# Two token blocks and the first weight slice of the second layer's projections fetched, split and multiplied during the last output tile of the first layer

## What is computed

```python
for i in range(DEPTH):                       # two layers, D_MODEL = 1024
    hp = rms_norm(xp, norm_g[i])
    if i % 2 == 0:
        zp = hp @ w_in_pool[j]               # 1024 x 4096
        br_p = pool_mix(u_p_ext, pos_p, w_pool_grp[j], pool_scale[j])
    else:
        zp = hp @ w_in_sb[j]                 # 1024 x 7168
        br_p = stick_breaking(q_p, k_p, v_p, pos_p, pos_p, sb_bias[j])
    xp = xp + merge_out(br_p, gate_p, mq_p, mg_p, mk_p, mv_p, mem_q_g[i], w_out[i])
```

## Time and profile before

| | us |
|---|---|
| three runs | 2331.37, 2334.16, 2334.32 |
| median | 2334.16 |
| profiled execution | 2338.4 |
| its span | 2336.7 |
| TensorE busy in the span | 2201.2 (94%) |
| mean granted TensorE clock | 0.971 |

### The profile page before, as it was taken

One profiled execution on the slowest core, in us unless ns is written; L12 is line 12 of the kernel. 1 busy time (PEld: TensorE's weight loads), 2 busy tenths in 40 slices (PEclk: granted clock), 3 DMA queues, 4 the chain that ended last, 5 costly groups with the idle time before them and its releaser, 6 DMA issues. The chain is left out here.

```text
span 2336.7 us, 47103 instructions
## 1 busy us (share of the span) xinstructions
PE 2201.2 (94%) x18709; PEld 1834.6 (79%) x18709; DVE 1292.6 (55%) x2040; ACT 1009.2 (43%) x2090; POOL 433.0 (19%) x542
## 2 busy tenths in 40 slices
PE   7799999997999689999999998889999999998999
PEld 6799899886688589999999997766666566654787
DVE  6846666435422374334444443588888888875211
ACT  7533223215311144333333343457777777775100
POOL 0533223202000043222222221321121111100000
PEclk9899999998899889999999999889999999999999
DMA  8222222144635553334433336789999999978331
GB/s 289 86 87 89 79 64 66 66 166 163 210 119 155 146 186 102 109 99 133 153 106 109 96 96 234 253 292 379 396 407 393 406 395 388 375 284 307 123 108 55
DMA packets 283274, 453.98 MB, mean 194 GB/s; under 512 B 30962, under 2 KB 208062, under 8 KB 283038
## 3 DMA queue, kind: packets, MB, share of 16 engines
q1 hardware_dynamic: 274958, 421.83, 51.8%
q0 software_dynamic: 8000, 29.10, 3.3%
q10 hardware_dynamic: 96, 0.02, 0.0%
HBM read 372.43 MB, written 78.43 MB: 193 GB/s over the span
## 5 line engine op out<-in xcount | busy, mean ns | idle before, releaser
L233 DVE TENSOR_TENSOR h_w_lo<-l_w,h_w_hi 128x512 fp32r<-128x512 f32 x264 | 213.7, 811 | 221.2 <-ACT h_w_hi L226 218.7
L226 ACT ACTIVATE h_w_hi<-l_w 128x512 fp32r<-128x512 f32 x264 | 166.7, 633 | 239.9 <-PE i_c L322 81.4
L320 PE MATMUL i_x<-h_t_hi,h_w_hi 128*128 128x264 f32 x560 | 163.3, 292 | 6.8 <-DVE h_t_lo L279 6.8
L2960 PEld LDWEIGHTS b_krow<-ar_arena,b_qd 128*32 128x32 f32 x3072 | 107.2, 111 | 72.6 <-issue 57.0
L192 POOL TENSOR_TENSOR h_w_lo_full<-l_w 128x512 f32<-128x512 f32 x44 | 57.5, 1308 | 560.5 <-DMA l_w<-in_w_in_sb_dram 229.9
L320 PE MATMUL i_y<-h_t_hi,h_w_hi 128*128 128x264 f32 x560 | 161.3, 288 | 0.0
L322 PE MATMUL i_x<-h_t_hi,h_w_lo 128*128 128x264 f32 x560 | 161.0, 287 | 0.0
L321 PE MATMUL i_x<-h_t_lo,h_w_hi 128*128 128x264 f32 x560 | 160.4, 286 | 0.0
L321 PE MATMUL i_y<-h_t_lo,h_w_hi 128*128 128x264 f32 x560 | 159.0, 284 | 0.0
L322 PE MATMUL i_y<-h_t_hi,h_w_lo 128*128 128x264 f32 x560 | 158.9, 284 | 0.0
L2960 PE MATMUL b_krow<-ar_arena,b_qd 128*32 128x128 f32 x3072 | 140.7, 279 | 7.9 <-ACT b_kev L2666 6.9
(11 more groups left out here) (368 smaller groups left out, 6424.9 us busy)
## 6 DMA issues: line engine op xcount, KB each, us to landing
ar_arena<-in_cache_sb_k_dram SPq DMA_DIRECT2D x73, 768.0 KB, 9.7
bf_vpage<-in_cache_sb_v_dram SPq DMA_DIRECT2D x64, 768.0 KB, 8.8
b_vpage<-in_cache_sb_v_dram SPq DMA_DIRECT2D x64, 768.0 KB, 8.5
l_w<-in_w_in_sb_dram SPq DMA_DIRECT2D x56, 512.0 KB, 3.9
l_w<-in_cache_sb_k_dram SPq DMA_DIRECT2D x36, 768.0 KB, 9.4
l_w<-in_w_in_pool_dram SPq DMA_DIRECT2D x32, 512.0 KB, 4.2
bf_kpage<-in_cache_sb_k_dram SPq DMA_DIRECT2D x19, 768.0 KB
ar_arena<-scratch_yT SPq DMA_DIRECT2D x14, 1024.0 KB, 6.6
```

The source lines that it names most:

```text
L226: act.activation(self.w_hi[:, i % RING, :, :], self.source(i), ACT.Copy).then_inc(self.high, 1)
L233: dve.tensor_tensor(self.w_lo[:, i % RING, :, :], self.source(i), self.w_hi[:, i % RING, :, :].bitcast(F32), ALU.subtract).then_inc(self.r ...
L320: pe.matmul(out, w_hi, t_hi, start=kk == 0 and x in ("P1", "P2", "P5"), stop=False, skip_group_check=True)
L2960: ins = pe.matmul(krow[pair * CT:(pair + 1) * CT, 0:P], qd[:, i % 2, at:at + CT], kt[u % 2][:, h, f, :], start=odd == 0 and f == 0, stop=o ...
```

## The change

Blocks 0 and 1 and slice a of the second layer's first pair are loaded by SyncE in the output phase, in the turn of tile 7 behind that tile's `load_other`. New places in SBUF are given to them, at addresses that tile 7 reads no more once its third weight row has been used (semaphore `dead`). ScalarE and VectorE round and split the two blocks and the weights of P1 and P2 at the end of the turn of tile 6. TensorE does P1 and the first half of P2 between the last output product and the transposes of tile 7, and the second half of P2 behind them. The order of the first pair becomes P1, P2, P5, and `in_phase` begins with P5. There the list of loads is shorter by slice a and blocks 0 and 1, and slice a of the second pair no longer waits for the split of the P3 weights, since the first pair's a lies elsewhere. The PSUM banks are allocated once for both phases. The first layer's own projections keep their order.

```diff
         self.seq = []
         for p in range(self.n):
-            self.seq += [(p, "P5")] + [(p - 1, "P4")] * (p > 0) + [(p, x) for x in ("P1", "P2", "P6", "P3", "P7")]
+            begin = [(p, "P5"), (p - 1, "P4"), (p, "P1"), (p, "P2")] if p else [
+                (0, x) for x in (("P1", "P2", "P5") if i else ("P5", "P1", "P2"))]
+            self.seq += begin + [(p, x) for x in ("P6", "P3", "P7")]
...
+    def place_early(self, top, bottom):
+
+        self.top, size = top, 4 * K2 * HALF
+        at = lambda name, shape, dt, offset: self.nc.alloc_sbuf_tensor_at(f"{self.k.tag}{name}", shape, dt, offset=offset)
+        for n in range(2):
+            self.full[n] = at(f"t_lo{n}_full", [P, K2, HALF], F32, top - size * (n + 1))
+            self.lo[n] = at(f"t_lo{n}", [P, K2, HALF], F32R, top - size * (n + 1))
+            self.hi[n] = at(f"t_hi{n}", [P, K2, HALF], F32R, top - size * (n + 3))
+        ring = [P, PLACES, 2, K2, P]
+        where = top - 4 * size - 4 * PLACES * 2 * K2 * P
+        full, rounded = at("w_full", ring, F32, where), at("w", ring, F32R, where)
+        self.w_full, self.w_hi, self.w_lo = full[:, :, 1], rounded[:, :, 0], rounded[:, :, 1]
+        self.wa0 = at("wa0", [P, KD, P], F32, bottom)
+
+    def wa_of(self, p):
+
+        return self.wa0 if self.i and p == 0 else self.wa
...
     def allocate_banks(self, k):
-        self.x, self.cbank = [k.ps("x", 2), k.ps("y", 2)], k.ps("c", 2)
+        banks = k.ps("bank", 8)
+        self.cbank, self.x, self.aux = banks[2:4], [banks[0:2], banks[4:6]], banks[6:8]
...
         col = self.columns[p][0]
-        if p:
+        if p > self.i:
             sp.wait_ge(self.rest, self.at[p - 1, "P3"] + 1)
...
+        if (self.i, p, x) == (1, 0, "P5") or (x == "P1" and (p or self.i == 0)):
...
-        bank = k.ps("bank", 4)
-        sbank = k.ps("sbank")
+        bank, sbank = (q.x[0] + q.cbank, q.x[1][0]) if q else (k.ps("bank", 4), k.ps("sbank"))
...
                         if t >= 4:
                             norm.load_other(sp, t)
+                        if t == N - 1:
+                            sp.wait_ge(s["ready"], 2 * (N - 1))
+                            sp.wait_ge(s["dead"], 1)
+                            q.load_a(sp, 0)
+                            for n in range(2):
+                                q.token_fetch(sp, S["tok"], n)
...
                         norm.evacuate(act, TILES, 0)
+                    if norm and t == N - 2:
+                        act.wait_ge(s["dead"], 1)
+                        act.wait_ge(s["ready"], 2 * (N - 1))
+                        act.wait_ge(s["ylo"], N)
+                        for n in range(2):
+                            q.round(act, n)
+                            q.token_high(act, n)
 
...
                         norm.sums(dve, TILES)
+                    if norm and t == N - 2:
+                        for n in range(2):
+                            q.remainder(dve, n)
+                            q.token_rest(dve, n, n + 1)
...
                                 ins.then_inc(s["ready"], 1)
+                            if norm and (t, at, half) == (N - 1, SPLIT, 1):
+                                ins.then_inc(s["dead"], 1)
                 if norm:
+                    pe.wait_ge(s["added"], 2 * (N - 1))
+                    q.product(pe, 0)
+                    pe.wait_ge(s["sadded"], 1)
+                    q.product(pe, 1, range(1))
                     norm.turn(pe, N - 1)
+                    q.product(pe, 1, range(1, 2))
 
...
                 q.load_b(sp, 0)
                 for n in range(2):
                     q.token_fetch(sp, S["tok"], 5, slice(n * SUB, (n + 1) * SUB))
-                q.load_a(sp, 0)
-                for t in (0, 1):
-                    q.token_fetch(sp, S["tok"], t)
                 q.load_b(sp, 1)
                 for t in (4, 2, 3, 6):
                     q.token_fetch(sp, S["tok"], t)
...
                             act.wait_ge(s["turned"], 6 * turns.index(p - 2) + 6)
                     q.copy(act, p, "P5", place(p, 1, 1), ACT.Copy)
-                q.round(act, 0)
+                q.round(act, 2)
                 for n in range(2):
                     q.token_high(act, 5, slice(n * SUB, (n + 1) * SUB))
-                q.round(act, 1)
-                q.token_high(act, 0)
-                q.round(act, 2)
-                q.token_high(act, 1)
                 q.round(act, 3)
                 for i, (p, x) in enumerate(q.seq):
...
                     dve.wait_ge(s["turned"], 3 * r + 3)
                     dve.tensor_copy(new[:, r % 2, :], aux[0][0:SAMPLES, 0:P]).then_inc(s["rowed"], 1)
-                q.remainder(dve, 0)
+                q.remainder(dve, 2)
                 for n in range(2):
-                    q.token_rest(dve, 5, n + 1, slice(n * SUB, (n + 1) * SUB))
-                q.remainder(dve, 1)
-                q.token_rest(dve, 0, 3)
-                q.remainder(dve, 2)
-                q.token_rest(dve, 1, 4)
+                    q.token_rest(dve, 5, n + 3, slice(n * SUB, (n + 1) * SUB))
                 q.remainder(dve, 3)
...
-                for i, (p, x) in enumerate(q.seq):
+                for i, (p, x) in list(enumerate(q.seq))[2:]:
...
```

More of the change, by code:

```diff
@@ L105, in __init__ @@
         self.nc, self.k, self.i, self.src, self.columns, self.n = nc, k, i, src, columns, len(columns)
-        self.full, self.lo = [], []
-        for n in range(7):
-            self.allocate_tokens(n)
-        self.w_hi = k.sb("w_hi", [P, RING, K2, P], F32R)
-        self.w_full, self.w_lo = self.two_kinds("w_lo", [P, RING, K2, P])
-        self.wb = [c["w"][:, :, n * P:(n + 1) * P] for n in range(2)]
-        self.wa = c["w"][:, :, 2 * P:3 * P]
+        self.ring = PLACES
+        self.ahead = self.ring - 1
+        self.full, self.lo, self.hi = [None] * 7, [None] * 7, [None] * 7
         self.loaded_b = [k.sem(f"loaded_b{n}") for n in range(2)]
@@ L140, in allocate_tokens @@
         full, lo = self.two_kinds(f"t_lo{n}", [P, K2, HALF])
-        self.full.append(full)
-        self.lo.append(lo)
+        self.full[n], self.lo[n] = full, lo
     def raw(self, q, half):
@@ L217, in round @@
         p, x = self.seq[i]
-        if i >= RING:
-            act.wait_ge(self.done, 2 * (i - RING) + 2)
+        if i >= self.ring:
+            act.wait_ge(self.done, 2 * (i - self.ring) + 2)
         if x in ("P1", "P2"):
@@ L296, in tokens_vector, with product @@
             self.token_rest(dve, t, n)
-    def product(self, pe, i):
+    def product(self, pe, i, halves=range(2)):
         p, x = self.seq[i]
@@ L302, in product @@
         t = self.TOKENS[x]
-        for n in range(2):
+        rests = {"P1": 1, "P2": 2, "P5": 3} if self.i else {"P5": 1, "P1": 3, "P2": 4}
+        rests.update({"P6": 5, "P3": 6, "P7": 7, "P4": 8})
+        for n in halves:
             if p == 0:
-                pe.wait_ge(self.t_rest, {"P5": n + 1, "P1": 3, "P2": 4, "P6": 5, "P3": 6, "P7": 7, "P4": 8}[x])
+                pe.wait_ge(self.t_rest, rests[x] + n * (x == "P5"))
             if x == "P5" and p:
@@ L1065, in _ @@
                 memory.place("mp")
-                for j in range(AHEAD - 1):
+                for j in range(q.ahead - 1):
                     q.loads(sp, j)
@@ L1070, in _ @@
                 for i, (p, x) in enumerate(q.seq):
-                    q.loads(sp, i + AHEAD - 1)
+                    q.loads(sp, i + q.ahead - 1)
                     if x == "P4" and p < 4:
@@ L1151, in _ @@
                 q.tokens_scalar(act, 0)
-                for j in range(6, AHEAD):
+                for j in range(6, q.ahead):
                     q.round(act, j)
                 for i, (p, x) in enumerate(q.seq):
-                    q.round(act, i + AHEAD)
+                    q.round(act, i + q.ahead)
                     kind_a, _, kind_b, _ = POOL_KINDS[p]
@@ L1244, in _ @@
                             mix(n - 1)
-                    q.remainder(dve, i + AHEAD)
+                    q.remainder(dve, i + q.ahead)
                     if x == "P2":
@@ L2142, in _ @@
             def _(gp):
-                for j in range(AHEAD + 1):
+                for j in range(q.ahead + 1):
                     q.combine(gp, j)
                 for i, (p, x) in enumerate(q.seq):
-                    q.combine(gp, i + AHEAD + 1)
+                    q.combine(gp, i + q.ahead + 1)
                     if (p, x) in ((0, "P4"), (1, "P4")):
```

94 lines of the change are left out of this document (63 added, 31 removed).

## The result

The changed kernel took 2340.72 us (median of 12 runs, 2334.98 to 2347.49); the kernel before took 2332.93 (12 runs, 2328.36 to 2342.81). The ratio is 1.0037, with a 95% interval of 1.0024 to 1.0051: 8.6 us slower (5.6 to 11.9).

A forecast was written before the change was run, and what follows sets the result against it. TensorE, busy 94%, loses time at idle or low-clock places, notably between the first layer's output and second layer's projections. Shift + 13.2 less 7.5 from fewer loads gives + 5.7 on 2334.16: 2339.9 us, range 2332.5 to 2344.0.

The forecast's parts named there:

- the band of + 3.9 to + 8: Whole kernel: the main forecast's range of slowdown in us against the kernel before, chance 0.57.
- The shift, 13.2: Output phase: tile 7's adds wait behind the splits, 12.9 plus 0.3, so the projections' first load starts 13.2 us later.
- the upper bound 15.4: Output phase: slowest case of the hold, block 0 landing 9.3 us after issue, shift 15.4 us.
- The 0.3 for TensorE's lateness: Tile 7's transposes: P1 and half of P2 stand ahead, making TensorE up to 0.7 us late, taken as 0.3.
- `load_a(1)` at S + 21.6: Projections: with three transfers gone, this slice lands 21.6 us after the projections' first load, instead of 29.1.
- P7 stays the last wait, and the anchor is S + 32.9: Projections: P7 waits last; the second pair's P5 starts 32.9 us after the projections' first load, P7 at low clock.
- The term of 7.5: Projections: two blocks (5.6) and a slice (1.9) off the load list gain 7.5 us, bounds 6.5 and 8.5.
- P7's low clock: Projections: P7 was assumed to keep running at the 1.2 GHz level, 0.22 us a matmul against 0.12 afterwards.
- Nothing behind the anchor: After the second pair's P5 starts: TensorE runs without gaps at 0.98 of the clock, so no term was counted.
- Rival 1: Projections: P7 finds the full clock and 2.5 us return, + 3.2, 2337.4 us; chance 0.2 together with favourable bounds.
- Rival 2: Output phase: new loads are slow, sharing the queue with tile 6's stores and tile 7's loads; + 9.6, 2343.8 us; chance 0.1.
- Rival 3: Output phase: loads land before tile 7's adds are held; with no hold at all - 7.5, 2326.7 us; chance 0.1.
- Rival 4: Projections gain nothing because the products were never the bound; only the shift remains, + 13.2, 2347.4 us; chance 0.03.

The follow-up runs named there:

- e4: The changed kernel run again with nothing altered, for a second trace: 2341.39 us.
- e8: The kernel before run again with nothing altered, for a second trace: 2336.59 us.
- e7: e1 with the copy of P5's result moved ahead of the rounding that waits for `load_a(1)`: 2326.67 us, 0.9972 of the kernel before.
- e1: Changed kernel with SyncE's three output-phase loads issued ahead of tile 6's store: 2328.73 us, 0.9987 of the kernel before.
- e6: Kernel before with token blocks rounded and split ahead of the weights in steps 2 and 3 of the projections: 2332.38 us, 1.0000.
- e10: Kernel before with weights 8 to 13 rounded and split behind the token blocks of steps 4 to 6: 2327.56 us, 0.9983.
- e2: Changed kernel with loads kept in the output phase, but splits, P1 and P2 returned to the projections' start: 2329.44 us, 0.9999 of the kernel before.

## Why the prediction was right, and which term was mis-sized

**Direction and mechanism were right.** Two terms of opposite sign, and the hold wins. The sum was + 5.7; the marks and the runs say + 8.6, which is above the band of + 3.9 to + 8 that had the largest chance. That the time itself came within 0.8 us of the 2339.9 forecast is in part luck: the sum started from 2334.16, the median of three runs, and that of twelve is 1.2 lower.

**The shift, 13.2.** Measured 28.34 - 14.62 = 13.7, and 13.7 again in the other pair, e4 less e8. The parts: the loads left as written, 1.01 behind tile 7's `load_other`. ScalarE's timeline has the slice and the two blocks in:

```profile
788.46 0.63 ACT L269 ACTIVATE h_w<-h_wa 128x512 fp32r<-128x512 f32 x1 [14.23 <-DMA h_wa<-in_w_in_sb_dram]
791.41 1.96 ACT L317 ACTIVATE h_t_hi<-h_t_lo_full 128x2112 fp32r<-128x2112 f32 x1 [2.33 <-DMA h_t_lo_full<-scratch_tok]
...
794.11 1.96 ACT L317 ACTIVATE h_t_hi<-h_t_lo_full 128x2112 fp32r<-128x2112 f32 x1 [0.21 <-DMA h_t_lo_full<-scratch_tok]
...
834.94 0.63 ACT L269 ACTIVATE h_w<-l_w 128x512 fp32r<-128x512 f32 x1 [4.70 <-DMA l_w<-in_w_in_sb_dram]
835.47 0.65 ACT L374 ACTIVATE i_stage<-h_bank 128x264 f32<-128x264 f32 x2
```

Blocks 8.4 and 11.1 behind the first load's issue (forecast 7.3 and 10.1), 2.7 apart (2.8). So the adds were held 14.2, between the forecast 12.9 and the upper bound 15.4. The rest of the chain gave 0.5 back: adds to S took 14.7 against 15.2, since the turn followed the adds by 4.55 against 4.48 and the transposes took 1.04 against 1.59, at a granted clock of 1.00 behind the products against 0.64 behind 3.91 of idle time. The 0.3 for TensorE's lateness was not needed. The adds did not pass the splits, though VectorE stood idle for 8.35 while they were ready. The Trainium skill (TensorE: Matmul & The Clock Gate, Architectural detail) has the queues of ScalarE and VectorE as strict FIFO; the trace agrees.

**`load_a(1)` at S + 21.6.** Its rounding starts at 834.94, S + 21.7. The three transfers left the list as worked out. The price that the prediction took from the Trainium skill (DMA: Bandwidth & Descriptors, Anatomy of one DMA) is the page's fit for single DMAs that GpSimd issues. Here SyncE issues them, and the two blocks came 2.7 apart, as in the rows of before.

**"P7 stays the last wait, and the anchor is S + 32.9".** This step failed in its mechanism. P7 started at 840.55 without a wait and at the full clock (granted 1.00); TensorE then stood 3.46 for VectorE's add of P3, and the anchor came at S + 33.9. VectorE's timeline:

```profile
835.60 1.20 DVE L276 TENSOR_TENSOR h_w<-l_w,h_w 128x512 fp32r<-128x512 f32 x1 [1.42 <-ACT h_w L269]
838.02 2.43 DVE L322 TENSOR_TENSOR h_t_lo<-h_t_lo_full,h_t_hi 128x2112 fp32r<-128x2112 f32 x1 [1.21 <-ACT h_t_hi L317]
840.37 1.28 DVE L276 TENSOR_TENSOR h_w<-l_w,h_w 128x512 fp32r<-128x512 f32 x2
841.58 3.43 DVE L322 TENSOR_TENSOR h_t_lo<-h_t_lo_full,h_t_hi 128x2112 fp32r<-128x2112 f32 x1
844.93 1.75 DVE L276 TENSOR_TENSOR h_w<-l_w,h_w 128x512 fp32r<-128x512 f32 x1
846.60 0.76 DVE L382 TENSOR_TENSOR i_stage<-h_bank,i_stage 128x264 f32<-128x264 f32 x2
```

The chain from the slice's rounding to the anchor is rounding, block 3, block 6, a remainder, the add: 847.17 - 834.94 = 12.2 after, and 12.2 in e4. Before it was already there: 12.4 in e8, and 850.84 - 839.49 = 11.35 in the first trace, where the remainder ahead of the add took 0.68 and not 1.75. In that trace VectorE's timeline has the add just ahead of the anchor, where the slow P7 ended too, and so it stayed hidden. In e8, whose P7 ran at the full clock from S + 34.9, TensorE shows the same wait of 3.46 for it. VectorE before, then TensorE in e8:

```profile
850.27 0.76 DVE L337 TENSOR_TENSOR i_stage<-i_c,i_stage 128x264 f32<-128x264 f32 x2
```

```profile
840.29 0.36 PE L320 MATMUL i_x<-h_t_hi,h_w_hi 128*128 128x264 f32 x1 [1.84 <-DVE h_t_lo L279]
...
846.91 0.36 PE L320 MATMUL i_c<-h_t_hi,h_w_hi 128*128 128x264 f32 x1 [3.46 <-DVE i_stage L337]
```

So the anchor moved with the slice, by 29.1 - 21.7 = 7.4. In the first pair of traces 0.9 of it is missing, since the chain before happened to be that much shorter: 40.4 - 33.9 = 6.5. In the other pair it is 41.5 - 34.1 = 7.4. The term of 7.5 was nearly right, though P7 is not what carried it: the add hangs on the same landing. Two smaller misses went with it. P3 started at S + 22.7, not 20.4: the copy of P5 (835.47) stood behind the rounding that waits for the slice. I had quoted this pattern from the earlier trace rows and counted the copy in P7's chain, but not ahead of P3; e7 shows S + 20.6 with the copy moved. And P7's low clock, which I carried over, went away.

**Nothing behind the anchor.** This is the term that was mis-sized most. The sum had none there, on the ground that TensorE ran at 0.98 behind it before. After, 3.46 of idling stand directly ahead of it, and the windows read:

```profile
847.17:853.00 5.83, 5.83 (x26) 5.83 (x27) 2.07 (x5) 0.18 (x1) 1.28 (x1) 0.50 0.31 90
853.00:869.00 16.00, 16.00 (x135) 16.00 (x134) 6.83 (x8) 5.42 (x13) 7.58 (x6) 0.99 0.39 124
```

26 matmuls in 5.83 us, at the 1.2 GHz level; at the 0.12 us of the prediction they take 3.1. From the anchor to the mark it is 24.97 against 22.50 before, + 2.5. The low clock left P7 and came back behind the point at which I stopped counting. In the other pair it is 23.56 against 22.26, + 1.3. Over all fourteen traces this stretch takes 22.2 to 22.5 where TensorE waited less than 0.8 at the anchor, and 23.6 to 25.0 in the six where it waited 2.59 to 6.25 and the granted clock then fell to 0.50. The exception is e8: it waited 3.46 like the changed kernel, but the granted clock stayed at 1.00 and the stretch took 22.3. Why is open.

The three stretches are parts of one interval, so they must add up: 13.7 - 6.5 + 2.5 = 9.7 in the first pair of traces, 13.7 - 7.4 + 1.3 = 7.6 in the other. That their mean is the 8.6 of the runs to the tenth is luck with two traces each. Term by term, against the forecast's 13.2 - 7.5 + 0 = 5.7: the shift was 0.5 larger, the gain up to the anchor 7.0 on average (0.5 smaller), and the term put at nothing was 1.9 on average.

**Rivals.** Rival 1 (P7 at the full clock) came true in its place, and the idle stretch ahead of P7 that was held against it was gone. It did not bring its 2.5, because the anchor waits for the add (as it did in e8), and the low clock behind the anchor cost 1.3 to 2.5. Rival 2's slow transfers came by half: the adds were held 14.2, where the forecast had 12.9 and this rival 15.4. Rival 3's turning point is shown by e1: with the split ending 0.9 behind E7 the result is on the other side, by 4.8 at the mark (3.0 by the runs, not clear of noise) and not the 7.5 worked out; the wait at the anchor (2.59) and the low clock behind it (23.8 to the mark) are in it too. Against rival 3 stood 3.40 for the issue of the two blocks; in the output phase it took 1.50. Rival 4 is excluded by the way from S to the anchor: 33.9 and 34.1 in the two traces of the changed kernel, 40.4 and 41.5 before. (The lower end of the range, 2332.5, is 1.5 under what its own source, rival 1 with good bounds, sums to.)

## What to carry to other kernels

Work that is moved ahead of a chain's first instruction on an in-order engine holds the chain until its data have landed and it has run; here 8.35 of the 14.2 us were waiting and 5.83 were work. Ask when the data land, and issue these loads ahead of everything that can wait, or put the work behind the chain. Once a wait is shortened, look along every queue for whatever waits for the same landing: the next one (here an add that frees a PSUM bank) may have been hidden behind the first by chance. Don't end the sum at a point because the clock was full there before: where a wait moved to the anchor, the clock behind it was mostly, but not always, at the low level. And take a second trace of the kernel before ahead of calling one wait the last; here e8 would have shown the add.

## What the runs showed of the hardware

**The front part spreads more than the difference sought.** E7 lies at 795.79 and 790.39 in two traces of the same kernel, at 789.69 and 789.55 in its variants e6 and e10, and from 784.94 to 793.41 in ten traces of the changed one and its variants, where little ahead of it differs. Why is open; the marks, counted from E7, agree within 1.3 us for one kernel.

**VectorE beside GpSimd.** The two halves of block 5's split take 2.45 us before; after, with slice a already in SBUF, GpSimd combines weights at that time, and they take 4.57. With the remainder ahead of them (1.20 against 0.69) this put P5 at S + 9.5 and not 8.3. VectorE before, VectorE after, GpSimd after:

```profile
817.32 2.45 DVE L279 TENSOR_TENSOR h_t_lo<-h_t_lo_full,h_t_hi 128x1056 fp32r<-128x1056 f32 x2 [0.28 <-ACT h_t_hi L274]
```

```profile
820.29 4.57 DVE L322 TENSOR_TENSOR h_t_lo<-h_t_lo_full,h_t_hi 128x1056 fp32r<-128x1056 f32 x2
```

```profile
819.90 1.60 POOL L243 TENSOR_TENSOR h_wa<-l_w 128x512 f32<-128x512 f32 x1
821.58 2.17 POOL L247 TENSOR_TENSOR h_wa<-h_wa 128x512 f32<-128x512 f32 x1
823.71 2.29 POOL L235 TENSOR_TENSOR h_w_full<-l_w 128x512 f32<-128x512 f32 x1
```

The same combination of GpSimd takes 1.26 in the earlier trace rows, and again at 817.21 after, both with VectorE idle, and 2.29 here. VectorE's split of block 1 takes 2.35 in the output phase of the changed kernel, with GpSimd idle, and 3.44 in e2, where it runs from 809.62 on while GpSimd combines weights. The Trainium skill (GPSIMD Engine Reference, Key points) has GpSimd share its SBUF interfaces with VectorE, with contention from VectorE instructions that have two SBUF inputs, as this split has; the trace agrees. No run took GpSimd's work away at this place and left all else, so the cause is argued and not shown.
